# Feed-forward of a two-layer diffusion trunk: first product as seven block products, second product pair by pair

## The reference

```python
def sq_relu_mlp(h, w1, w2):
    return jnp.square(jax.nn.relu(h @ w1)) @ w2

    hp = modulate(rmsnorm(xp, norm_ffn_pre[layer]), mod_p[3], mod_p[4])
    hs = modulate(rmsnorm(xs, norm_ffn_pre[layer]), mod_s[3], mod_s[4])
    xp = xp + mod_p[5] * rmsnorm(sq_relu_mlp(hp, w_ffn_in[layer], w_ffn_out[layer]), norm_ffn_post[layer])
    xs = xs + mod_s[5] * rmsnorm(sq_relu_mlp(hs, w_ffn_in[layer], w_ffn_out[layer]), norm_ffn_post[layer])
```

## Time and profile before

| | us |
|---|---|
| median of three runs | 1446.57 (1444.94 to 1447.14) |
| span of the profiled execution | 1446.1 |
| PE busy | 1400.9 |
| DVE, ACT, POOL busy | 689.8, 538.4, 566.7 |
| chain that ended last: share on PE | 80% |

### The profile page before, as it was taken

The page is one execution under the profiler, slowest core; times in us unless marked ns, Lnnn a source line. Parts: engine busy times, 40 slices in busy tenths (PEclk is TensorE's granted clock), DMA queues, the critical chain, the costliest instruction groups (busy, mean ns, idle before and its releaser), DMA issues.

```text
span 1446.1 us, 19826 instructions
## 1 busy us (share of the span) xinstructions
PE 1400.9 (97%) x7958; PEld 1205.4 (83%) x7958; DVE 689.8 (48%) x1235; ACT 538.4 (37%) x920; POOL 566.7 (39%) x443
## 2 busy tenths in 40 slices
PE   5999999999999999999999999999999999999998
PEld 2876777899899898898777867788998998988986
DVE  4477854532535535435864588526222222222236
ACT  4376824622132131231551467646321311312322
POOL 1431414354253253243342577543532532532440
PEclk9999999999999999999999999999999999999999
DMA  9534273342343233333155100043422222212201
GB/s 353 152 98 145 64 257 117 117 110 80 103 131 130 89 117 117 115 119 116 59 202 183 59 1 1 2 150 125 122 85 73 88 80 67 88 62 85 88 29 73
DMA packets 95027, 153.77 MB, mean 106 GB/s; under 512 B 10764, under 2 KB 49368, under 8 KB 94936
## 3 DMA queue, kind: packets, MB, share of 16 engines
q1 hardware_dynamic: 83296, 146.74, 30.8%
q10 hardware_dynamic: 11640, 5.76, 1.6%
HBM read 149.58 MB, written 2.92 MB: 105 GB/s over the span
## 4 chain that ended last, share of the span: by engine, by line
PE 80%; DVE 6%; ACT 3%; issue 2%; POOL 2%; DMA 1%; DVEq 0%; ACTq 0%; POOLq 0%
PE PS L1695 24%; PE PS L1697 24%; PE PS L1696 24%; PE PS L2008 1%; PE PS L1997 1%; DVE X L1410 1%; PE PS L1746 1%; PE PS L1844 1%; PE PS L1976 1%; DMA GG<-gates 1%; PE PS L1977 1%; POOL GG L1221 1%; ACT XCB L1022 0%; POOL WHF L1221 0%; PE PS L1953 0%
## 5 line engine op out<-in xcount | busy, mean ns | idle before, releaser
L1254 POOL TENSOR_TENSOR WL<-RAW,WH 128x512 fp32r<-128x512 f32 x340 | 461.5, 1392 | 702.8 <-ACT WH L961 685.6
L1695 PE MATMUL PS<-HH,WH 128*128 128x384 f32 (+1 forms) x1152 | 357.2, 310 | 1.3 <-DVE HL L1429 1.3
L1697 PE MATMUL PS<-HH,WL 128*128 128x384 f32 (+1 forms) x1152 | 355.5, 309 | 0.0
L1696 PE MATMUL PS<-HL,WH 128*128 128x384 f32 (+1 forms) x1152 | 355.5, 309 | 0.0
L961 ACT CAST WH<-RAW 128x1024 fp32r<-128x1024 f32 x170 | 169.5, 1048 | 388.7 <-PE PS L1697 338.0
L1695 PE MATMUL PS<-WH,AH 128*128 128x512 f32 x640 | 250.2, 391 | 0.6 <-DVE AL L1471 0.4
L1697 PE MATMUL PS<-WH,AL 128*128 128x512 f32 x640 | 249.6, 390 | 0.0
L1696 PE MATMUL PS<-WL,AH 128*128 128x512 f32 x640 | 249.4, 390 | 0.0
L1695 PEld LDWEIGHTS PS<-HH,WH 128*128 128x128 f32 x1152 | 218.2, 189 | 6.8 <-issue 3.5
L1696 PEld LDWEIGHTS PS<-HL,WH 128*128 128x128 f32 x1152 | 218.4, 190 | 0.6
L1697 PEld LDWEIGHTS PS<-HH,WL 128*128 128x128 f32 x1152 | 218.2, 189 | 0.0
(11 more groups left out here) (236 smaller groups left out, 1621.4 us busy)
## 6 DMA issues: line engine op xcount, KB each, us to landing
RAW<-in_w_mod SPq DMA_DIRECT2D x32, 1024.0 KB, 5.2
RAW<-in_w_ffn_in SPq DMA_DIRECT2D x32, 1024.0 KB, 5.5
RAW<-in_w_ffn_out SPq DMA_DIRECT2D x32, 1024.0 KB, 4.7
RAW<-in_w_in_even SPq DMA_DIRECT2D x7, 1024.0 KB, 5.2
RAW<-in_w_qkv SPq DMA_DIRECT2D x6, 1024.0 KB, 5.8
MX<-in_w_mod SPq DMA_DIRECT2D x5, 1024.0 KB, 7.8
GG<-in_w_mod SPq DMA_DIRECT2D x5, 1024.0 KB, 8.4
EARLY_H<-in_w_mod SPq DMA_DIRECT2D x4, 1024.0 KB, 14.1
```

The source lines that it names most:

```text
L1254: ins = nc.gpsimd.tensor_tensor(cut(ring_view(WL, ld, j)), cut(w_view(ld, b)), cut(ring_view(WH, ld, j)).bitcast(f32), ALU.subtract)
L1695: MM(out, wh, xh, start=first, stop=False)
L1696: MM(out, wh, xl, start=False, stop=False)
L1697: return MM(out, wl, xh, start=False, stop=last)
```

## The change

**First product.** In each layer the 1024 × 4096 weight is taken in 16 pairs of tiles (256 features, 1024 rows: a 2 by 2 grid of blocks of 128 features by 512 rows), and the tokens in two halves of 320 columns by two halves of the width. Seven products P1 to P7 take the place of eight. Their weights are A11, A12, A22 and four sums S1 to S4 that DVE forms in place in the raw slot; their moving operands are blocks of the tokens and four sums T1 to T4 of all token tiles, formed by DVE once per layer (`comb`, three column parts), cast by ACT and cut by POOL. T2 and T4 lie where X lay: X is copied to memory at the start of the feed-forward and back after its last P3. Each product is 4 k-blocks × 3 matmuls of 320 columns in a bank. DVE and ACT join the products to four quarter tiles, square them and cut them in FH and FL.

**Second product.** It follows pair by pair: a group is two k-blocks of 512 columns; ten groups of the pair before stand behind the products of a pair, two behind each of the last five. The last two pairs' groups are done together at the end.

**Weights** are cut in units of 128 × 512 (12 slots, 11 units a pair), each placed by a rule behind a product or a group.

**Modulation.** All halves are matmul steps; one is loaded ahead for each of the first pairs, in places of its own (`ff_first`, `ff_second`).

The core of the diff:

```diff
 schedule()
+        w1_load(0)
+        w1_load(1)
+        product(0, "P1")
         T_(ph, TT - 2, cut=False, groups=True)
         step("norm", ph=ph, t=TT - 1)
         cut_()
+        step("comb", layer=layer, c=0)
+        product(1, "P1")
+        step("comb", layer=layer, c=1)
         T_(ph, TT - 1, groups=True)
+        product(0, "P2")
+        mod(*fill.pop(0))
+        w2_load(0)
+        step("comb", layer=layer, c=2)
+        product(1, "P2")
+        step("comblo", layer=layer)
+        flush()
+        for name in ("P6", "P5", "P7", "P4", "P3"):
+            product(0, name)
+        for p in range(PAIRS - 2):
+            asked = fill[0] + (mod_load(*fill.pop(0)),) if fill else None
+            w1_load(p + 2)
+            w2_load(p + 1)
+            q = 0
+            for name, ngroups in ((("P6", 0), ("P5", 2), ("P7", 3), ("P4", 3), ("P3", 2)) if p == 0 else
+                                  (("P1", 0), ("P6", 0), ("P2", 2), ("P5", 2), ("P7", 2), ("P4", 2), ("P3", 2))):
+                product(p + 1, name)
+                for _ in range(ngroups):
+                    group(p, q)
+                    q += 1
+                    if q == 2 and asked:
+                        mod(*asked)
...
+        for name in ("P1", "P6", "P2", "P5", "P7", "P4", "P3"):
+            product(PAIRS - 1, name)
+        for t in range(TT):
+            step("G2", uses_b=2, layer=layer, t=t, ph=ph + 1)
...
+        for p in range(2, PAIRS):
+            order += [(p, "A11"), (p, "A12"), (p, "S2"), w2[0], w2[1], (p, "S1"), (p, "A22"), (p, "S4"), w2[2], w2[3], (p, "S3")]
...
+OPERANDS = {"P1": ("A11", "B11"), "P2": ("A12", "B21"), "P3": ("S4", "B22"), "P4": ("A22", "T4"), "P5": ("S1", "T1"),
+            "P6": ("S2", "T2"), "P7": ("S3", "T3")}
+OUTPUT = {"P2": (0, 0), "P7": (1, 1), "P4": (1, 0), "P3": (0, 1)}
 SP
+                    elif place in ("ff_first", "ff_second"):
+                        if (ld["c"], ld["half"]) == (5, 0):
+                            upto(sp, b_ready, LAST_OUT[layer])
+                            upto(sp, b_free, LAST_OUT[layer])
+                            upto(sp, b_free, LAST_OUT[layer] - 1)
...
+                if ld["kind"] == "w2s" and ld["p"] == 0:
+                    for t in range(TT):
+                        sp.wait_ge(x_new, TT * 2 * ld["layer"] + t + 1)
+                        sp.dma_start(XD[t], X[:, t, :]).then_inc(x_out[t], 16)
...
+                    if old["kind"] in ("w1s", "w2s"):
+                        sp.wait_ge(u_lo, LAST_UNIT[RAW_LD[RAW_NO[i] - RAWN]])
...
+                if ld["kind"] == "w2s" and ld["p"] == PAIRS - 1:
+                    sp.wait_ge(p_done, PRODUCTS[ld["layer"], PAIRS - 1, "P3"])
+                    for t in range(TT):
+                        sp.dma_start(X[:, t, :], XD[t]).then_inc(x_back[t], 16)
 ACT
+                elif k == "comb":
+                    for i, name in enumerate(("T2", "T1", "T3", "T4")):
+                        act.wait_ge(t_add, 12 * layer + 4 * c + 4)
+                        nc.scalar.copy(SHI[name][:, :, PAIR_COLS[c]], SRAW[name][:, :, PAIR_COLS[c]]).then_inc(t_hi, 1)
+                elif k == "P":
+                    if name == "P1":
+                        act.wait_ge(p_done, s["count"] + 1)
+                        nc.scalar.copy(FZ[:, 2 * (p % 2) + 1, out_cols(0)], bank_of("P1", p)).then_inc(s1_copied, 1)
+                    elif name in OUTPUT:
+                        squared(layer, p, name)
...
+                casts(s)
 POOL
+                elif k == "comb":
+                    for i, name in enumerate(("T2", "T1", "T3", "T4")):
+                        if c == 2 and i < 2:
+                            continue
+                        pool.wait_ge(t_hi, 12 * layer + 4 * c + i + 1)
+                        nc.gpsimd.tensor_tensor(SLO[name][:, :, part], SRAW[name][:, :, part], SHI[name][:, :, part].bitcast(f32), ALU.subtract)
+                for u in s.get("cast", ()):
+                    pool.wait_ge(u_hi, u["number"] + 1)
+                    nc.gpsimd.tensor_tensor(unit_view(WLU, u), unit_raw(u["ld"], u["of"]), unit_view(WHU, u).bitcast(f32), ALU.subtract)
 DVE
+            def adds(s):
+                for u in s.get("add", ()):
+                    if name == "S1":
+                        raw_arrived(dve, u["ld"])
+                        V_.tensor_tensor(part("S1"), part("S1"), part("A22"), ALU.add).then_inc(s_add, 1)
+                        continue
+                    dve.wait_ge(u_lo, NUMBER[layer, p, {"S2": "A11", "S3": "A22", "S4": "A12"}[name]] + 1)
...
+                elif k == "comb":
+                    V_.tensor_tensor(in_pieces(z["T1"], c), in_pieces(late((0, 4)), c), early((0, 4)), ALU.subtract).then_inc(t_add, 1)
+                    for t in (0, 1, 2):
+                        dve.wait_ge(x_out[t], 16 * (layer + 1))
+                    V_.tensor_tensor(z["T2"], late((4, 8)), z["T1"], ALU.subtract).then_inc(t_add, 1)
+                    V_.tensor_tensor(z["T3"], late((4, 8)), late((0, 4)), ALU.subtract).then_inc(t_add, 1)
+                    for t in (3, 4):
+                        dve.wait_ge(x_out[t], 16 * (layer + 1))
+                    V_.tensor_tensor(in_pieces(z["T4"], c), early((4, 8)), in_pieces(z["T2"], c), ALU.subtract).then_inc(t_add, 1)
+                elif k == "P":
+                    if name == "P6":
+                        V_.tensor_tensor(u2, bank, s1, ALU.add).then_inc(u2_made, 1)
+                    elif name == "P7":
+                        V_.tensor_tensor(s1, bank, s1, ALU.add).then_inc(u3_made, 1)
+                        V_.tensor_tensor(c22, bank_of("P5", p), s1, ALU.add).then_inc(c22_made, 1)
...
 PE
+                elif k == "P":
+                    if name == "P1":
+                        if p == 0:
+                            pe.wait_ge(f_lo[0], 3 * layer + 3)
...
+                    u = s["unit"]
+                    pe.wait_ge(u_lo, u["number"] + 1)
+                    for kt in range(4):
+                        ins = split3(out, (wh[:, kt, :], wl[:, kt, :]), (xh[:, kt, :], xl[:, kt, :]),
+                                     kt == 0 and name not in ("P2", "P7", "P3"), kt == 3, name in ("P2", "P7", "P3"))
+                    ins.then_inc(p_done, 1)
+                elif k == "g":
+                    pe.wait_ge(ff_lo, RESTS[layer, p, "P4" if t < 2 else "P3"])
+                    b_acquire(b)
+                    for kt in (0, 1):
+                        pe.wait_ge(u_lo, u["number"] + 1)
```

More of the change, by code:

```diff
@@ L80, in mod, with apair @@
         nread[0] += 1
[L82 to L110, removed]
+    def apair(what, tile, src, col, ld=None, kh=0):
         if ld is None:
             ld = load("acols", src=src, col=col)
[L114 to L117, removed]
+        step("A", uses_a=2, frees=2, what=what, tile=tile, j=loads[ld]["first"], kh=kh)
     def bgroup(what, nb, t, j, ph=None):
@@ L170, in gate_in, with ffn, w1_load, w2_load @@
         step("gin", q=gate_no(layer, c, half), layer=layer, c=c, half=half)
-    def ffn(layer, fillers, ahead=None, vec=()):
-        fill, vec = list(fillers), list(vec)
+    funits, nproduct = [], [0]
+    def ffn(layer, fillers, ahead=None):
+        fill = list(fillers)
         ph = 1 if layer == 0 else 3
[L177 to L185, removed]
+        first_unit, done = 2 * n["block"], len(funits)
+        n["block"] += FFN_BLOCKS
+        last_out = [i for i, s in enumerate(steps) if s["kind"] == "B" and s["what"] == "wout" and s["ph"] == ph]
+        w1_ld, w2_ld = {}, {}
+        def w1_load(p):
+            w1_ld[p] = load("w1s", layer=layer, p=p)
+        def w2_load(p):
+            w2_ld[p] = load("w2s", layer=layer, p=p)
+        events = []
+        def product(p, name):
+            step("P", layer=layer, p=p, name=name, count=nproduct[0])
+            nproduct[0] += 1
+            events.append(len(steps) - 1)
+        def group(p, q):
+            step("g", uses_b=1, layer=layer, p=p, nh=q // TT, t=q % TT)
+            events.append(len(steps) - 1)
+        w1_load(0)
+        w1_load(1)
+        product(0, "P1")
         T_(ph, TT - 2, cut=False, groups=True)
@@ new lines, in ffn @@
+        index = lambda e: events[e] if e >= 0 else last_out[7 + e + 2]
+        for k, o in enumerate(order):
+            u = dict(layer=layer, slot=(first_unit + k) % UNITS, number=done + k, ld=w1_ld[o[0]] if len(o) == 2 else w2_ld[o[0]], of=o)
+            if k >= UNITS:
+                u["after"] = steps[events[used[order[k - UNITS]]]]
+            else:
+                u["after"] = steps[last_out[TT - 1 if k < 4 else -1]]
+            funits.append(u)
+            steps[index(place[o])].setdefault("cast", []).append(u)
+            if o[-1] in ("S2", "S3", "S4"):
+                steps[index(max(place[o] - 1, -1))].setdefault("add", []).append(u)
+            elif o[-1] == "A11":
+                steps[index(place[o])].setdefault("add", []).append(dict(layer=layer, ld=u["ld"], of=(o[0], "S1")))
```

(3 more changed lines are left out.)

721 lines of the change are left out of this document (416 added, 305 removed).

## The result

The changed kernel takes 1533.83 us (median of four runs, 1531.43 to 1534.08) against 1446.86 for the kernel before (four runs, 1444.94 to 1447.80): a ratio of 1.0598, with an interval of 1.0583 to 1.0613. It is 87.0 us slower; 1453 was forecast, 1425 to 1475 the range. The sign was right, the size far off. The profiled execution has a span of 1529.6 us and a mean granted clock of 0.972, where the kernel before had 1446.1 and 0.994.

The account below looks back on a forecast made before the run. TensorE, busy 97% of the span, was taken to bound the kernel. Terms −56.2 + 8 + 8 + 40 + 5 + 2 = +7 us on 1446.1, plus 0.5 to the median, gave 1453 us, range 1425 to 1475.

Parts of the forecast that it names:

- The matmuls: First product: 2688 matmuls of 320 columns at 0.1467 us replace 1536 pairs at 0.2933, −56.2 us.
- Rival 4: First product: a matmul floor near 0.17 us would make seven products cost as eight; called excluded, no chance given.
- The modulation halves: Six layer 1 modulation vectors move from VectorE sums to full matmul steps on TensorE, +8 us.
- The step that failed: Inside each pair: S3's slot frees at 4.4 us, load lands at 10.0, late eviction costs 0.4 us, +8 in all.
- rival 2: First product's single raw weight slot: a later remainder or load costs each of 28 pairs 1 us, 1481; chance 0.15.
- The term of +8: Wait for the fourth group's bank inside pairs: 0.4 us in 20 of 28 pairs, +8 us.
- The upper bound that I had worked out, +42: Inside pairs: if VectorE's sums also take the next queue place, 1.5 us in each of 28, +42.
- Pairs of over 27 us: Pair length named as showing the prediction wrong; 26.3 us in layer 1 would show it right.
- The start: Each feed-forward's start: X copies land at 277.5, GpSimd's remainders hold P7 to 296.3; 19.9 us idle a layer, +40.
- the 47 of starts, first pairs and ends: Waits at feed-forward starts +40, first-pair second-product weights behind them +5, layer ends +2 us.
- Rival 1: Feed-forward start covered better: hole about 8 us a layer, 1421, or 1437 at half; chance 0.28, nearly whole saving 0.03.
- Rival 3: Clock falls at each start, products behind the hole run at half speed, 2 × 5 us: 1463; chance 0.1.

Follow-up runs that it names:

- e3: Changed kernel with VectorE forming S1 after the second group's eviction and S2 after the fourth's: 1489.84 us, ratio 1.0301.
- e1: Changed kernel with SyncE issuing the second product's weight load only once the first product's has landed: 1505.89 us, ratio 1.0406.
- e10: GpSimd's ten remainders of the token sums given to VectorE, on a kernel combining several earlier edits: 1466.69 us, 4.0 below that kernel.
- e2: Changed kernel with VectorE forming S1 after the second group's eviction instead of before it, S2 following at once: 1552.40 us, ratio 1.0718.

## Why the prediction was wrong

**The matmuls: right.** The distance of starts in a product is 1.76 / 12 = 0.147 us, the midpoint that was taken from the earlier trace rows. A full pair is 26.04 for 25.92, which over 28 pairs is 3.4 us of the 56.2. Rival 4 had nothing for it. **The modulation halves: nearly right.** In e3 a pair with a step takes 28.55 us, 2.5 more than without: 6 × (2.5 − 0.7) = +10.9 for +8.

**The step that failed** is the time of one load and what waits behind it: S3's slot is free 4.4 us into the pair, "and the next megabyte lands 5.5 us later, at 10.0", and from it "0.4 us a pair where no modulation step lies between, 20 of 28 pairs: +8". The 4.4 was right: 4.56 by the rows. The load takes 6.6 us and lands 11.2 into the pair, because SP issues a second one 0.4 us behind it; the earlier trace rows gave the median of the kernel before, and e1, where no second load runs beside it, gives that time back (5.45). Against rival 2 I wrote that this load's time hardly varies in the rows. That is so in the median, but the trace of the kernel before has the case itself. There one such load in each feed-forward has a second one issued 0.4 us behind it, and takes 6.8 us in layer 0 and 6.6 in layer 1. SP, then the issues of that stretch (KB, us to landing):

```profile
278.48 0.37 SPq L919 DMA_DIRECT2D RAW<-in_w_ffn_in  x1
```

```profile
RAW<-in_w_ffn_in SPq DMA_DIRECT2D x1, 1024.0 KB, 6.8
RAW<-in_w_ffn_out SPq DMA_DIRECT2D x1, 1024.0 KB, 8.9
```

VectorE's sum then stops PE for 1.44 us, and S2's sum, which the forecast had in the evictions' way only at its upper bound, for 0.35 more. The term of +8 measures +44.0 (e3). Rival 2 had the mechanism and its condition ("a landing later than 10 us into the pair"), but I gave it a chance of 0.15 and a price of 1 us a pair; the rows say 1.57 in the mean over 28. The upper bound that I had worked out, +42, was close, and I took a value near the lower one. Pairs of over 27 us, which the prediction named as a sign of being wrong, are what the kernel after has. What I should have looked at was that SP's order puts both loads behind one free slot.

**The start: right in shape, short in size.** The copies land at 278.19 for 277.5. The chain behind them was walked at 0.69 us for a sum of VectorE and 1.33 to 1.39 for a remainder of GpSimd, side by side. They do not run side by side at those times. VectorE's sums, differences and products of the kernel after, sorted by whether GpSimd is busy during the whole of them (mean us, count in brackets): two operands in SBUF, 512 columns with an fp32 result, 0.69 (37) alone and 1.26 (48) beside; remainders of 320 columns 0.48 (42) and 1.37 (75); one operand in PSUM, 512 columns, 0.684 (116) and 0.681 (81). So of these only the ones with both operands in SBUF are slowed. GpSimd is slowed as well: its remainders of 512 columns take 1.29 us (39) alone, 1.29 (113) beside operations of VectorE that read PSUM, and up to 1.73 beside the others at the start. e10 shows that taking GpSimd out gives VectorE its 0.69 back. The earlier trace rows had a sign of it: the group L1566 has a median of 692 and a longest of 1482 ns. By the Trainium skill (SBUF — State Buffer, Who interferes with whom) VectorE and GpSimd share a pair of ports under an exclusive lock, which an operation of VectorE with one operand in PSUM does not need; the counts agree. So does the pace: from 256 to 512 columns alone VectorE's time grows from 0.42 to 0.69 us and GpSimd's from 0.72 to 1.28, so the part that goes with the columns is 0.54 and 1.12 us of a 512-column operation, an estimate from these times. Their sum is 1.66, and at the start one of each comes every 1.67 us (289.62 to 291.29, above). P7 comes 5.3 us later than forecast: +11 in two layers. In the forecast P7 waits for S3's remainder, and that one did end 4.4 us late, at 300.71. But P7 waited for nothing by then: it follows P6 and P5, and of its delay the slow clock of P6 (3.10 us for 1.76, and 3.18 in layer 1) makes up some 0.8 us. The first two pairs behind it take 36.45 us for 32.3: +8.

**What was not counted at all** is the state's store of four-byte pieces in front of a load that is now on the path, with two other long pairs in e3: 30.09 and 30.76 us. With that of 35.67 they lie 11 to 16 us over their neighbours (26.04 or 28.55).

The sum: −56.2 + 3.4 + 10.9 + 44.0 = +2.1, and the 47 of starts, first pairs and ends + 11 + 8 + (11 to 16) = 77 to 82; together 79 to 84 of 87.0 measured. The rest of 3 to 8 I have not placed; there may be overlap among the terms, and what slowed the first two pairs was not tested by itself. Rival 1 fell: the start was not covered. Rival 3's clock was seen at both starts, but not with its price of 5 us each: P6 alone ran slow on the path, and P7 had the full clock again. No run changes the clock alone; after the start its slow stretches lie inside the terms above.

## What to carry to other kernels

When work moves onto an engine that evicts, write its program order for one stage out, and for each instruction that waits for a transfer name the eviction behind it; the price is what the bank's owner loses, not the wait's total. Take a load's time from rows in which the same neighbours are under way, and ask what else is issued behind the same slot. Two engines that each look half idle can still slow each other: before one counts their operations as parallel, look at the longest of a group, not its median.

## What the chip showed that was not expected

- VectorE's operations with two SBUF operands and GpSimd's beside them take up to two and a half times as long (0.69 to 1.74 us, 512 columns), and GpSimd's 1.29 become 1.71; with one operand of VectorE's in PSUM neither shows it (0.684 and 0.681; GpSimd's 1.29 and 1.29).
- A store of 1024 pieces of four bytes holds the megabyte load issued behind it: 12.6 to 13.2 us where it is 5.3 alone.
- In e2 every second hole of about 2 us in PE was followed by a granted clock of 0.52 over the 2.4 us shown, with PE fully busy; holes as long in the pairs between were not. What decides it stays open.
